# Query tiles loaded three positions earlier, convolved halves later; one tanh tile and four low-probability buffers

## What is computed

```python
# (A) attention: 8 query heads over 2 key heads of 64, softmax over selected keys
logits = jnp.where(valid, einsum(q_b, k_sel) * att_scale, NEG_INF)
p = softmax(logits);  y = einsum(p, v_sel)
# (B) mLSTM: short causal convolution on q and k, SiLU, then a scan over chunks
qk = silu(causal_depthwise_conv(concat([mq, mk]), w_conv, b_conv))
mq, mk = split(qk, 2);  hm = mlstm_chunkwise(mq, mk, mv, i_pre, f_pre)
y_mlstm = sigmoid(mo) * rmsnorm(hm)
```

## Time and profile before

| | |
|---|---|
| median of 3 runs | 3360.48 us (3359.68 to 3360.97) |
| the profiled execution, its own time | 3364.48 us |
| its span, first to last instruction | 3362.9 us |
| mean granted TensorE clock | 0.944 of full speed |
| TensorE matmul busy over the span | 2964.8 us, 88% |
| VectorE busy | 2596.7 us, 77% |
| ScalarE busy | 1988.9 us, 59% |
| the changed stage, about | 1180 to 1885 us of the span |

### The profile page before, as it was taken

The page is one execution under the profiler, slowest core; times in us unless marked ns, Lnnn a source line. Parts: engine busy times, 40 slices in busy tenths (PEclk is TensorE's granted clock), DMA queues, the critical chain, the costliest instruction groups (busy, mean ns, idle before and its releaser), DMA issues. The chain is left out here.

```text
span 3362.9 us, 46383 instructions
## 1 busy us (share of the span) xinstructions
PE 2964.8 (88%) x13280; PEld 2276.3 (68%) x13280; DVE 2596.7 (77%) x3864; ACT 1988.9 (59%) x2851; POOL 566.4 (17%) x720
## 2 busy tenths in 40 slices
PE   7998899899899956888889789998499999999990
PEld 5766778678678633555566567777388888888870
DVE  6577589899999966888885544442899999999985
ACT  5322467587678445677667533332477777777770
POOL 0211110100000052444333100000111111111115
PEclk9999999999999967999999889999699999999995
DMA  3222533233212255546334466552478879667868
GB/s 125 88 69 76 146 102 127 92 121 97 63 60 76 67 138 133 126 102 117 108 71 66 131 194 187 169 162 99 178 287 321 315 287 352 241 253 258 309 247 338
DMA packets 378860, 546.04 MB, mean 162 GB/s; under 512 B 32528, under 2 KB 213440, under 8 KB 378576
## 3 DMA queue, kind: packets, MB, share of 16 engines
q1 hardware_dynamic: 346368, 434.02, 42.1%
q0 software_dynamic: 28448, 100.94, 8.0%
q10 hardware_dynamic: 3888, 9.18, 0.7%
HBM read 510.70 MB, written 138.19 MB: 193 GB/s over the span
## 5 line engine op out<-in xcount | busy, mean ns | idle before, releaser
L915 DVE TENSOR_TENSOR e_w_lo<-e_raw,e_w_hi 128x1024 fp32r<-128x1024 f32 x386 | 446.4, 1216 | 4.2 <-ACT e_w_hi L772 4.2
L1585 PE MATMUL x_ps<-h_hi,w_hi 128*128 128x512 f32 (+1 forms) x992 | 390.7, 394 | 6.1 <-PEq L90 5.0
L1585 PE MATMUL x_ps<-h_lo,w_hi 128*128 128x512 f32 (+1 forms) x992 | 388.8, 392 | 0.0
L1585 PE MATMUL x_ps<-h_hi,w_lo 128*128 128x512 f32 (+1 forms) x992 | 388.3, 391 | 0.0
L772 ACT CAST e_w_hi<-e_raw 128x1024 fp32r<-128x1024 f32 x386 | 377.0, 1055 | 5.6 <-PE e_pG L710 5.6
L1772 DVE TENSOR_SCALAR_CACHE_REDUCE x_relu<-x_score,x_cand 128x1024 uint8<-128x1024 f32 (+3 forms) x217 | 315.6, 1486 | 3.6
L1687 ACT ACTIVATE x_relu<-x_score,x_cand 128x896 int8<-128x896 f32 (+3 forms) x217 | 281.0, 1296 | 59.6 <-DVE x_cand L1779 59.2
L2451 DVE CUSTOM_DVE_ANT_0 t_junk<-t_L,t_mask 128x512 bf16<-128x512 f32 (+3 forms) x320 | 186.2, 604 | 106.2 <-PE t_L L2201 97.8
L2421 ACT ACTIVATE t_probT<-t_ST 128x512 f32<-128x512 f32 x272 | 161.4, 593 | 164.8 <-PE t_ST L2230 153.9
L710 PE MATMUL e_pG<-e_w_hi,e_x_hi 128*128 128x512 f32 x768 | 246.7, 403 | 3.6 <-DVE e_x_lo L910 3.6
L710 PE MATMUL e_pG<-e_w_lo,e_x_hi 128*128 128x512 f32 x768 | 242.2, 397 | 0.0
(11 more groups left out here) (422 smaller groups left out, 6848.3 us busy)
## 6 DMA issues: line engine op xcount, KB each, us to landing
e_raw<-in_w_exp_gate SPq DMA_DIRECT2D x392, 256.0 KB
e_raw<-in_w_exp_up SPq DMA_DIRECT2D x392, 256.0 KB
e_raw<-in_w_exp_down SPq DMA_DIRECT2D x192, 512.0 KB
projT<-x_out SPq DMA_DIRECT2D x120, 256.0 KB, 3.0
slot_out<-e_y POOLq DMA_DIRECT2D x48, 512.0 KB, 5.9
w_raw<-in_w_in SPq DMA_DIRECT2D x40, 512.0 KB, 5.3
o_gate<-projT SPq DMA_DIRECT2D x32, 512.0 KB
slot_out<-x_zeros SPq DMA_DIRECT2D x31, 512.0 KB
```

Source lines behind the costliest of these rows:

```text
L915: nc.vector.tensor_tensor(w_lo[:, u, :], raw[:, u, :], w_hi[:, u, :].bitcast(F32), ALU.subtract).then_inc(gl, 1)
L1585: last = nc.tensor.matmul(ps[0:w, u % 4, :], wt[:, m % 2, kk, 0:w], ht[:, kk, q * 512:(q + 1) * 512], start=(kk == 0 and s == 0), stop=(kk ...
```

## The change

`load(n + 4)` now comes one position after the second step of tile n has ended, ahead of the stores, and waits for TensorE's last `logits_t` of that step (semaphore `st_ok`). `load_chunk` is split: the two parts from `projT` stay where they were, and the two from `qkT` with their waits are a function `load_convolved`, two positions later; for chunk 0 three positions later, and chunk 1's loads and rows move from f = 23 to f = 29. `TH` has one buffer, and the tanh waits for the product of the unit before. The low probabilities have four buffers in place of three. Line numbers behind line 1968 are 3 to 13 higher in the new file.

```diff
-        PH, PL = sb("probT_hi", [P, LAG + 1, 512], F32R), sb("probT_lo", [P, LAG - 1, 512], F32R)
+        PH, PL = sb("probT_hi", [P, LAG + 1, 512], F32R), sb("probT_lo", [P, LAG, 512], F32R)
...
-        U, TH = sb("v_U", [P, 3, HALO + 512]), sb("v_T", [P, 2, 512])
+        U, TH = sb("v_U", [P, 3, HALO + 512]), sb("v_T", [P, 512])
...
+                for z, row in ((2, C_MV), (3, C_MO)):
+                    sp.dma_start(X[:, b, z, :, :], pg.d["projT"][row:row + MH * MD, at].rearrange("(h p) n -> p h n", p=P)).then_inc(x_in[b], 16)
+
+            def load_convolved(k):
+                b, at = k % 2, slice(k * P, (k + 1) * P)
                 for s in range(3):
                     sp.wait_ge(c_st[s], 16 * units_before(s, 2 * MH * (k // 4 + 1)))
                 for z in range(2):
                     sp.dma_start(X[:, b, z, :, :], qk_d[z * MH:(z + 1) * MH, :, at].rearrange("h p n -> p h n")).then_inc(x_in[b], 16)
...
+                k = chunk_at(f, -11)
+                if k and k > 1:
+                    load_convolved(k)
...
                 if f == CHUNK0 - 9:
                     load_chunk(0)
+                if f == CHUNK0 - 6:
+                    load_convolved(0)
+                if f == CHUNK0 - 3:
                     load_chunk(1)
+                    load_convolved(1)
                     load_rows(1)
...
             for f in range(FLAT + 20):
+                s = ended(f, 1)
+                if s is not None and STEPS[s][1] == 1 and STEPS[s][0] + 4 < NT:
+                    n = STEPS[s][0]
+                    sp.wait_ge(st_ok, at_st[s, n] + 1)
+                    load(n + 4)
                 s = ended(f, LAG)
                 if s is not None:
                     store(s)
                     n, v = STEPS[s]
-                    if v == 1 and n + 4 < NT:
-                        load(n + 4)
...
-                    if j >= 2:
-                        act.wait_ge(cy_ok, j - 1)
-                    a.activation(TH[:, j % 2, :], CY[:, j % 3, :], ACT.Tanh).then_inc(th_ok, 1)
+                    if j >= 1:
+                        act.wait_ge(cy_ok, j)
+                    a.activation(TH[:, :], CY[:, j % 3, :], ACT.Tanh).then_inc(th_ok, 1)
...
-                if f >= LAG - 1:
-                    dve.wait_ge(pv_ok, f - LAG + 2)
+                if f >= LAG:
+                    dve.wait_ge(pv_ok, f - LAG + 1)
```

More of the change, by code:

```diff
@@ L1971, in load_chunk @@
                     sp.dma_start(X[:, b, z, :, :], qk_d[z * MH:(z + 1) * MH, :, at].rearrange("h p n -> p h n")).then_inc(x_in[b], 16)
-                for z, row in ((2, C_MV), (3, C_MO)):
-                    sp.dma_start(X[:, b, z, :, :], pg.d["projT"][row:row + MH * MD, at].rearrange("(h p) n -> p h n", p=P)).then_inc(x_in[b], 16)
             def load_rows(k):
@@ L2243, in values @@
                 pe.wait_ge(pl_ok, f + 1)
-                nc.tensor.matmul(O[0:AD + 1, :, :], VH[:, j, v, :], PL[:, f % (LAG - 1), :], start=False, stop=(j == n)).then_inc(pv_ok, 1)
+                nc.tensor.matmul(O[0:AD + 1, :, :], VH[:, j, v, :], PL[:, f % LAG, :], start=False, stop=(j == n)).then_inc(pv_ok, 1)
             def side(f):
@@ L2455, in probabilities_low @@
                 dve.wait_ge(ph_ok, f + 1)
-                if f >= LAG - 1:
-                    dve.wait_ge(pv_ok, f - LAG + 2)
-                v_.tensor_tensor(PL[:, f % (LAG - 1), :], PT[:, f % 4, :], PH[:, f % (LAG + 1), :].bitcast(F32), ALU.subtract).then_inc(pl_ok, 1)
+                if f >= LAG:
+                    dve.wait_ge(pv_ok, f - LAG + 1)
+                v_.tensor_tensor(PL[:, f % LAG, :], PT[:, f % 4, :], PH[:, f % (LAG + 1), :].bitcast(F32), ALU.subtract).then_inc(pl_ok, 1)
             def negated(s, seen):
@@ L2515, in side @@
                     dve.wait_ge(th_ok, j + 1)
-                    v_.scalar_tensor_tensor(out=CY[:, j % 3, :], in0=TH[:, j % 2, :], scalar=1.0, in1=CY[:, j % 3, :],
+                    v_.scalar_tensor_tensor(out=CY[:, j % 3, :], in0=TH[:, :], scalar=1.0, in1=CY[:, j % 3, :],
                                             op0=ALU.add, op1=ALU.mult).then_inc(cy_ok, 1)
```

## The result

| | kernel before | the change |
|---|---|---|
| median, five runs each on one chip | 3360.97 us (3359.68 to 3363.04) | 3342.13 us (3336.07 to 3342.48) |
| ratio, 95% interval | | 0.994 [0.9929, 0.9951] |
| the profiled execution, its own time | 3364.48 us | 3336.07 us |
| its span | 3362.9 us | 3334.5 us |
| mean granted TensorE clock in it | 0.944 | 0.952 |

Faster by 18.8 us in these runs, where 22.6 was forecast. The profiled execution of the change is the fastest of its five, so its 28 us against the profiled execution of before is not the change's gain.

The account below looks back on a forecast made before the run. The stage was taken as engine-bound except for two holes where TensorE waits for queries. Query loads 23.3, tanh tile -1.2 and low buffer +0.5 sum to 22.6 us, from 3360.5 to 3338 us, range 3329 to 3345.

Parts of the forecast that it names:

- second rival: Chunk 0's convolved parts land no earlier than before, at 1309.27; gain 18.5 us, time 3342 us; chance 0.20.
- What bounds it: The stage is bound by engines except in two holes, 8 and 22 us; 29.9 us of query waits in reach.
- Tiles 4 and 5: Earlier query loads remove TensorE's waits of 7.19 and 0.61 us; together 7.8 us gained.
- Tile 7, step by step: Earlier load(7) removes the 22.10 us wait; a new one at f = 29 keeps 6.6; 23.3 us with tiles 4, 5.
- stands behind the broadcast rows: Reason given for unit 7's late store: queued behind the rows, landing 17.4 us after the rows' issue.
- The split: Later convolved halves of chunks 2 to 15: some 20 us for a landing of at most 5.4, so nothing.
- One tanh tile: Tanh also waits for VectorE's previous product at units 1, 3, 5 and 7; -1.2 us, bounds 0 and 2.7.
- Fourth low buffer: VectorE's 29.6 us of free-buffer waits in 1770 to 1890; gain +0.5 us, bounds 0 and 4.6.
- The clock did not stay up: Rival: all 29.9 us of query waits go and TensorE's clock stays up; 3330 us; chance 0.17.
- As late as before: Rival: chunk 0's convolved parts land at 1309.27, f = 31 begins at 1310.5; 3342 us; chance 0.20.
- Hole renamed: Rival: most of the 22 us becomes a wait on ACT; gain below 6.7 us, about 3355; chance 0.05.
- slower: Rival: the single tanh tile serialises ACT and VectorE in the stage; 3378 us; chance 0.03.

Follow-up runs that it names:

- e9: The change, unaltered, run a third time beside later variants on one chip: median 3339.62 us, ratio 0.9932.
- e2: The change without its two tile edits (two tanh buffers, three low-probability buffers), leaving only SP's new order: 3339.88 us, ratio 0.9935.
- e3: The kernel before with only the query loads moved earlier, chunk transfers in the old order: 3347.92 us, ratio 0.9963.
- e4: The change with chunk 0's two broadcast rows issued from ACT's queue instead of SP's: 3336.38 us, ratio 0.9939.
- e8: The change with each chunk's broadcast rows stored side by side, one 2 KB piece per partition's copy: 3337.44 us, ratio 0.9938.
- e12: The kernel before with only the broadcast rows stored side by side, no transfer at another position: 3342.53 us, ratio 0.9943.
- e7: The kernel before with only the single tanh tile and its wait: 3361.18 us, ratio 1.001.
- e6: The change with three low-probability buffers instead of four, the single tanh tile kept: 3341.26 us, ratio 0.9951.
- e10: The change with broadcast rows side by side, run again beside the unaltered change on one chip: 3337.03 us, ratio 0.9929.

## Why the prediction was right, step by step

The forecast was 3338 us with 3329 to 3345; the result is 3342.1, inside, and the change's 16 executions in three series have a median of 3338.7 us (3332.6 to 3344.3). The 4 us between forecast and result is in no step up to f = 36: even e9's profiled execution of 3344.33 us is within 0.6 us of the first trace there. The time alone would not have told the forecast from its second rival, which also gave 3342 us; the traces do, below.

- **What bounds it.** Right: the holes were all there was to gain. Behind f = 64 nothing changed (455.8 us against 455.2), and from f = 210 to the end it is 106.2 us in both.
- **Tiles 4 and 5, 7.8 us.** Right. By f = 26 the ruler shows 8.1, 6.7 and 8.0 us in the three traces of the change, and 8.2 and 9.6 in e2 and e3, without the tile edits. It was most doubtful as a sum of waits, since VectorE was 91% busy behind them, yet nothing took them back.
- **Tile 7, step by step.** Counted from f = 0 of each execution: rows issued at 63.4 us (forecast 61.7), convolved parts issued at 79.6 (80.2), TensorE at f = 31 at 87.2 (87.7). ACT waits 4.01 us (5.3), TensorE 6.85 (6.6). The gain at f = 36 is 23.8 us, against 23.3 - 1.2 forecast up to there. One count was wrong: nine transfers now stand between the rows and the convolved parts, seven more than before, and not five.
- **Its reason was only half right.** The prediction said that unit 7's store "stands behind the broadcast rows" in the queue. e4 refutes SP's queue: with the rows in another one it is the same. They hold up SP's transfers from there too, and SP's issues (5.71 us for two), and e8 and e12 show that it comes with the rows' layout. The number came out because it was taken from a row, 17.4 us, and not from the story. It would have misled anyone who had moved the rows to another queue.
- **The split, costed at nothing.** Wrong by omission. For chunks 2 to 15 "nothing" fits: from f = 64 to the end e2, with the split, takes 455.4 us and e3, without it, 456.0. For chunk 0 the split, with chunk 1 moved behind, keeps an output store from going out behind the parts, which is 7.66 us of TensorE in e3. In the sum it cancelled, since I reckoned with the finished order and not with the loads alone.
- **One tanh tile, -1.2 us.** Right in place (four tanhs wait for the product). Its size isn't shown: e7 is 1.9 us late at f = 20 and 0.4 at f = 26, with a scatter of 1.4, and e6, which keeps the single tile, is as early as the kernels with two. Nothing here contradicts -1.2, and nothing measures it.
- **Fourth low buffer, +0.5 us.** Mis-sized: nothing in the stretch it was meant for, the lower bound. VectorE lost 29.6 us of waits on TensorE, and 29.2 us of waits on ACT stand there now, while the stretch takes as long. In the first 26 positions it may even cost something (e6 against the change), which the prediction did not weigh.
- **The rivals.** The clock did not stay up, with 6.85 us of wait or with e8's 2.90. "As late as before" fell, though the measured 3342.1 us is its number: the parts were there for ACT's tanh at 86.0 us after f = 0 (1303.95), where it began at 90.5 before (1309.27), and f = 31 begins at 87.2, where this rival had 91.8. "Hole renamed" and "slower" fell: TensorE is busy 20.32 of the old hole's 22 us, and e7's ratio is 1.001.

What went unpriced is the scatter. The change varies by 6 to 8 us within a series, in part through stretches like 1385 to 1405, where the change's clock is 1.00 in two traces and 0.79 in the third. What decides which it is in a given execution stays open.

## What to carry to other kernels

When a small transfer lands late, ask what else is under way on all DMA engines, and then what its bytes look like in memory, before its place in a queue. Here laying 8 KB-spaced rows side by side gained as much (20 us) as reordering a whole stage (19 to 24). Gains that close the same hole don't add up: with both, e8 and e10 stand 21 and 26 us below the kernel before. Read a gain of a few us by positions inside a profile, and stop at the first place where no edit can act any more: medians of five runs of the same program differed by 5 us.

## What the runs showed that I had not expected

- **The rows' copies are slow as a pattern, not as small pieces.** While they are under way, the DMA engines are busy 0.11 of their time at 37 GB/s, in the change 0.24 at 38. Two transfers of 256 KB take up to 17.9 us. But the convolved parts of `t_m_X` have the same shape, 128x4x128, and the same pieces of 512 bytes, and land in 2.8 to 6.2 us (line 1976; the `projT` parts that go out behind chunk 0's rows take up to 14.3). What differs is that all partitions read the same four rows, 8 KB apart. As one run of 2 KB, still read by all partitions, they take 3.7 to 8.2 us. Which of the two, the spacing or the number of pieces from one place, does it was not tried.
- **They hold up an engine's issues, of another queue too**: 3.3 to 3.9 us for one issue of SP (e4), 5.71 for two (the change).
- **The clock can fall behind a wait, not at it.** In e8 the first matmuls after a wait of 2.90 us take 0.39 to 0.58 us, and 1.3 us after its end they take 0.63; in the change they are slow at once (0.80, 0.65).
